# Expert weights of a two-layer backbone: ring of five tiles of each kind, two down tiles to a slot, the next unit's first three tiles fetched in the running unit

## The chip, the cores and the metric

The kernel runs on one core of one Trainium2 chip. The metric is the device time of one execution in microseconds. Three executions of the kernel before took 1493.27, 1498.73 and 1499.72 us (median 1498.73).

## The reference, cut to what matters

The program is one inference step of a two-layer backbone for 128 context tokens and 128 latent tokens of width 1024, all in 32-bit floats. Layer 0 mixes with a gated linear recurrence beside latent attention and a dense SwiGLU; layer 1 mixes with a bidirectional RWKV-7 recurrence and ends in a mixture of eight experts, two of which each token uses. Only that last part is touched:

```
def swiglu(x, wg, wu, wd):
    return (jax.nn.silu(x @ wg) * (x @ wu)) @ wd

def moe_swiglu(x, w_router, wg, wu, wd):     # 8 experts, D_FF_EXPERT = 2816
    logits = (xt @ w_router).astype(jnp.float32)
    top_v, top_i = lax.top_k(logits, TOP_K)                      # TOP_K = 2
    top_w = jax.nn.softmax(top_v, axis=-1)
    gate = jnp.sum(jax.nn.one_hot(top_i, N_EXPERTS) * top_w[..., None], axis=1)
    for e in range(N_EXPERTS):
        out = out + gate[:, e:e + 1] * swiglu(xt, wg[e], wu[e], wd[e])
```

## The kernel before, in words

The experts' stage works in units. A unit is one expert with up to 86 (CAP) of its tokens; there are as many units as experts (8) plus one for each expert that more tokens chose, a number that the kernel finds at run time and writes into a small table (TBL). With these inputs there are 8 units. The hidden width 2816 is cut into 22 tiles of 128 (HB). For tile t a unit needs one gate/up weight tile (1 MB, `("gu", t)`) and one down weight tile (0.5 MB, `("d", t)`).

TensorE's order in a unit (function `unit`, lines 1683 to 1771): gate/up 0 with the transposition of the previous unit's outputs between its halves (line 1666), gate/up 1, down 0, the slots (line 1673); then a hardware loop over LOOPS = 5 passes of ROWS = 4 tiles, each tile being gate/up t and then down t-1; then the gather of the next unit's tokens (line 1656) and down 21. Line 1691 is the matmul of gate and up (64 matmul records a tile), line 1715 that of down (32 records a tile). Units 1 to 6 are one hardware loop around this (line 1778), unit 0 and the last unit have code of their own. In unit 0 the first two passes of four tiles are written out and the loop runs from the third. ScalarE takes the silu (line 2252), VectorE the product (line 3216). Results alternate between two buffers by the parity of t.

SyncE issues every weight transfer (`expert_tiles`, lines 576 to 603), in the order of UNIT_TILES: gu 0, gu 1, d 0, then gu t and d t-1 in turn, then d 21. The weights go to 11 slots of 1 MB each ("ring"). Slots 0, 1 and 2 are kept for gu 0, gu 1 and for d 0 and d 21 (one half each); the other eight turn over, four for gate/up and four for down tiles, each down tile using half of its slot. SyncE waits before each transfer until both halves of TensorE's array have done with the tile that lies there (counters tile_used and tile_used0), then issues, and comes to the next tile in order. In unit 0 five tiles (gu 6, 7, 8 and d 5, 6; AHEAD) go to working arrays W6 to W9 that the layer before has left, once the residual is ready ("x" at 6). Counters slot3, slot4, ... tell TensorE that a slot's tile has landed.

Of the kernel before, what the change touches and what calls it, by code (L numbers as in the profile page):

```python
# [28 lines left out]
P = 128  # L29
# [19 lines left out]
ROWS, LOOPS = 4, 5  # L49
# [76 lines left out]
UNIT_TILES = [("gu", 0), ("gu", 1), ("d", 0)]  # L126
# [5 lines left out]
def moe_slot(kind, t):  # L132
    if kind == "gu":
        return EXPERTS[t if t < 2 else 3 + 2 * ((t - 2) % ROWS)]
    return EXPERTS[2 if t in (0, HB - 1) else 4 + 2 * ((t - 1) % ROWS)]


def moe_free(kind, t):

    taken = up_taken if kind == "gu" else down_taken  # L140
    if kind == "gu":
        return taken(t) - UT if t < 2 else taken(t - ROWS) if t >= 2 + ROWS else taken(t + ROWS * (LOOPS - 1)) - UT
    if t in (0, HB - 1):
        return taken(t) - UT
    return taken(t - ROWS) if t > ROWS else taken(t + ROWS * (LOOPS - 1)) - UT

# [49 lines left out]
def program(nc, t, out):  # L198
    ctx = ExitStack()
    with ctx:  # L200
# [210 lines left out]
        AHEAD = {("gu", ROWS + 2 + n): W[6 + n][:, :] for n in range(3)}  # L411
        AHEAD.update({("d", ROWS + 1 + n): W[9][:, n * D:(n + 1) * D] for n in range(2)})
        AHEAD_SLOTS = [moe_slot(kind, b) for kind, b in AHEAD]
        AHEAD_LANDED = 16 * (2 + len(AHEAD))
# [88 lines left out]
        def _(sp):  # L503
# [72 lines left out]
            def expert_tiles(u, e):  # L576

                for n, (kind, b) in enumerate(UNIT_TILES):
                    slot = ring[:, moe_slot(kind, b), :]
                    if kind == "gu":  # L580
                        dst, src = slot, t["moe_gu"][bass.ds(e, 1), b].rearrange("a p n -> (a p) n")
                    else:
                        dst = slot[:, D:2 * D] if b == HB - 1 else slot[:, 0:D]
                        src = t["moe_w_down"][0][bass.ds(e, 1), b * P:(b + 1) * P, :].rearrange("a k n -> (a k) n")
                    if u is None and (kind, b) in AHEAD:
                        sp.wait_ge(sem("x"), 6)
                        sp.dma_start(AHEAD[kind, b], src).then_inc(sem("x_in"), 16)
                        continue
                    free = n - RING + 1 if u is None and n < RING else moe_free(kind, b)
                    if u is None and (kind, b - ROWS) in AHEAD:  # L590
                        free = (up_taken if kind == "gu" else down_taken)(b - 2 * ROWS)
                    at = N_MOE + free if u is None else u * UT + (N_MOE + free)
                    sp.wait_ge(sem("tile_used"), at)
                    sp.wait_ge(sem("tile_used0"), at)
                    last = kind == "d" and b == HB - 1
                    sp.dma_start(dst, src).then_inc(sem("slot_last" if last else f"slot{moe_slot(kind, b)}"), 16)

            expert_tiles(None, 0)
            with sp.Fori(1, NE - 1) as u:
                expert_tiles(u, u)  # L600
            sp.wait_ge(sem("table"), 1)
            with sp.Fori(NE - 1, sp.value_load(TBL[0:1, UNITS:UNITS + 1], min_val=NE, max_val=UNITS)) as u:
                expert_tiles(u, sp.value_load(TBL[0:1, bass.ds(u, 1)], min_val=0, max_val=NE - 1))
# [89 lines left out]
        def _(pe):  # L693
# [985 lines left out]
            due0 = list(walk.due)  # L1679

            def unit(u, prev=None, rows=False):
# [13 lines left out]
                def gate_up(t, due, between=lambda: None, ahead=None):  # L1695

                    slot = moe_slot("gu", t)
                    if ahead is None:
                        pe.wait_ge(sem(f"slot{slot}"), due)
                    else:  # L1700
                        pe.wait_ge(sem("x_in"), AHEAD_LANDED)
                    w = (ring[:, slot, :] if ahead is None else ahead).rearrange("p (w k n) -> p w k n", w=2, k=KC)
                    across(bank[t % 2], w[:, 0])
                    between()
                    across(bank[2 + t % 2], w[:, 1])

                def down(t, arrived, due, hid, ahead=None):

                    if ahead is None:
                        pe.wait_ge(sem(arrived), due)  # L1710
                    pe.wait_ge(sem("hid"), hid)
                    half = D if t == HB - 1 else 0
                    w = ring[:, moe_slot("d", t), half:half + D] if ahead is None else ahead
                    for c in range(KC):
                        ins = [mm(bank[4 + c // 4][hp, (c % 4) * CAP:(c % 4 + 1) * CAP],  # L1715
                                  w[:, c * P + hp.start:c * P + hp.stop], HIDU[:, t % 2, :],
                                  start=t == 0 and c % 4 == 0, stop=t == HB - 1, skip_group_check=True) for hp in HALVES]
                        if prev is not None and t == HB - 1 and c % 4 == 3:
                            ins[0].then_inc(sem("last_down"), 1)
                            ins[1].then_inc(sem("last_down"), 1)  # L1720
                    if prev is None or t < HB - 1:
                        taken(ins)
# [8 lines left out]
                def once(slot):  # L1731
                    return u * 16 + (due0[slot] + 16)

                pe.wait_ge(sem("xg"), u * 2 + 2)
                gate_up(0, once(moe_slot("gu", 0)), outputs_turned)
                gate_up(1, once(moe_slot("gu", 1)))
                down(0, f"slot{moe_slot('d', 0)}", once(moe_slot("d", 0)), u * HB + (FT + 1))
# [9 lines left out]
                def due(slot, i, skipped):  # L1747

                    return u * (16 * LOOPS) + i * 16 + (due0[slot] + 16 - (16 if skipped and slot in AHEAD_SLOTS else 0))

                def steps(i, skipped, ahead={}):

                    for t in range(2, 2 + ROWS):
                        slot, slot_d = moe_slot("gu", t), moe_slot("d", t - 1)
                        gate_up(t, due(slot, i, skipped), ahead=ahead.get(("gu", t + ROWS)))
                        down(t - 1, f"slot{slot_d}", due(slot_d, i, skipped), u * HB + i * ROWS + (FT + t),
                             ahead.get(("d", t - 1 + ROWS)))

                if first_of_all:
                    steps(0, False)  # L1760
                    steps(1, False, AHEAD)
                with pe.Fori(2 if first_of_all else 0, LOOPS) as i:
                    steps(i, True)
# [7 lines left out]
                down(HB - 1, "slot_last", u * 16 + 16, u * HB + (FT + HB))  # L1771
# [22 lines left out]
        def _(act):  # L1794
# [448 lines left out]
            def unit(u, prev=None, rows=False):  # L2243
# [21 lines left out]
                with act.Fori(0, LOOPS) as i:  # L2265
                    for t in range(2, 2 + ROWS):
                        silu(t, u * UT + i * (3 * ROWS) + (N_MOE + gate_taken(t)), u * HB + i * ROWS + (FT + t - 1))
# [1118 lines left out]
```

## Time and profile before

| | |
|---|---|
| median of three executions | 1498.73 us |
| profiled execution | 1498.9 us, span 1497.0 us, mean granted clock 0.996 |
| TensorE busy | 1433.6 us, 96% |
| VectorE, ScalarE, GpSimd busy | 529.7, 303.5, 38.7 us |
| moved by DMA | 413.76 MB, mean 276 GB/s |
| lines 1691 and 1715, the experts' matmuls | 450.2 and 237.2 us busy |

The span is the time from the first to the last instruction of the profiled execution. Of the chain of work that ended last, 91% is TensorE, and 43% is lines 1691 and 1715. Busy times of TensorE overlap in part, since matmuls of the two halves of the array run together: 64 records of 238 ns take 2.39 us. Among the DMA queues q1 carries the weights, q0 the transfers of GpSimd, q8 and q14 are named "instruction".

### The profile page before, as it was taken

The numbers are of one execution on the slowest core, as the hardware profiler recorded it, in microseconds if no ns is written. First come the engines' busy times: TensorE is split into PE (matmuls) and PEld (weight loads), VectorE is DVE, ScalarE is ACT, GpSimd is POOL, SyncE is SP. The second block draws the span as 40 slices with busy tenths as digits, with TensorE's granted clock in tenths as the row PEclk, the third lists the DMA queues.
The fourth block names the chain that finished last, engine by engine and source line by source line (L and its number), as shares of the span: only waits on it lengthen the run. The fifth ranks groups of instructions, "written<-read, shape, count | busy, mean of one in ns | idle before, by whom it ended". The sixth has DMA issues, their size and how long they took to land.

```text
span 1497.0 us, 60951 instructions
## 1 busy us (share of the span) xinstructions
PE 1433.6 (96%) x27147; PEld 1274.0 (85%) x27147; DVE 529.7 (35%) x1496; ACT 303.5 (20%) x870; POOL 38.7 (3%) x59
## 2 busy tenths in 40 slices
PE   5999999999999999999999899999999999999997
PEld 3888588999547787888778899999999999999896
DVE  1474427666636355788623210000101010010012
ACT  2112423000102523455342010100101010000101
POOL 0100000000000000100000000000000000000000
PEclk9999999999999999999999999999999999999999
DMA  9823849544448132100185999999999999999995
GB/s 390 321 95 123 308 170 396 196 170 169 179 180 330 57 127 87 35 8 7 48 283 219 378 397 403 417 417 418 399 418 399 419 417 417 417 403 417 394 414 212
DMA packets 77441, 413.76 MB, mean 276 GB/s; under 512 B 12920, under 2 KB 13354, under 8 KB 40452
## 3 DMA queue, kind: packets, MB, share of 16 engines
q1 hardware_dynamic: 68752, 399.96, 67.4%
q0 software_dynamic: 7456, 9.56, 2.2%
q8 instruction: 98, 1.61, 0.4%
q10 hardware_dynamic: 1108, 2.41, 0.4%
q14 instruction: 27, 0.22, 0.0%
HBM read 407.50 MB, written 6.48 MB: 277 GB/s over the span
## 4 chain that ended last, share of the span: by engine, by line
PE 91%; DVE 3%; DMA 2%; ACT 2%; issue 1%; ACTq 0%; DVEq 0%; SPq 0%
PE banks L1691 29%; PE banks L1715 14%; PE banks L1070 9%; PE banks L1109 4%; PE banks L718 3%; PE banks L721 3%; PE banks L824 3%; PE banks L827 3%; PE banks L1236 2%; PE banks L1295 2%; PE banks L744 2%; PE banks L1656 1%; PE banks L1313 1%; PE banks L860 1%; PE banks L1324 1%
## 5 line engine op out<-in xcount | busy, mean ns | idle before, releaser
L1691 PE MATMUL banks<-w,ring 128*64 128x86 f32 x11072 | 450.2, 238 | 8.1 <-issue 5.1
L1691 PEld LDWEIGHTS banks<-w,ring 128*64 128x64 f32 x11072 | 426.6, 136 | 18.9 <-issue 7.5
L3216 DVE TENSOR_TENSOR w<-w,banks 128x86 f32<-128x86 f32 x176 | 43.1, 245 | 566.5 <-PE banks L1691 558.4
L1715 PE MATMUL banks<-w,ring 128*64 128x86 f32 x5568 | 237.2, 238 | 1.7 <-issue 1.5
L1715 PEld LDWEIGHTS banks<-w,ring 128*64 128x64 f32 x5568 | 219.4, 137 | 2.0 <-issue 2.0
L2252 ACT ACTIVATE w<-banks 128x86 f32<-128x86 f32 x176 | 42.7, 242 | 587.7 <-PE banks L1691 587.7
L718 PE MATMUL banks<-w,ring 128*128 128x256 f32 x224 | 49.2, 380 | 0.6 <-issue 0.3
L744 PE MATMUL banks<-ring,ct 128*32 128x256 f32 x768 | 47.3, 395 | 2.3 <-ACT ct L1818 2.1
L721 PE MATMUL banks<-ring,w 128*128 128x256 f32 x224 | 48.9, 379 | 0.0
L718 PEld LDWEIGHTS banks<-w,ring 128*128 128x128 f32 x224 | 42.3, 190 | 7.4 <-issue 1.8
L721 PEld LDWEIGHTS banks<-ring,w 128*128 128x128 f32 x224 | 42.3, 190 | 5.9 <-DVE w L2334 0.2
L1070 PE MATMUL banks<-w 128*128 128x128 f32 x352 | 43.0, 275 | 0.6 <-DVE w L2608 0.6
L824 PE MATMUL banks<-ht,ring 128*128 128x256 f32 x192 | 43.5, 383 | 0.0
L1070 PE MATMUL banks<-ht,ring 128*128 128x128 f32 x352 | 43.0, 275 | 0.0
L1070 PE MATMUL banks<-w,ring 128*128 128x128 f32 x352 | 42.9, 275 | 0.0
L744 PEld LDWEIGHTS banks<-ring,ct 128*32 128x32 f32 x768 | 23.6, 113 | 22.4 <-issue 6.6
L1109 PE MATMUL banks<-ring,w 128*128 128x512 f32 x88 | 42.2, 592 | 0.0
L827 PE MATMUL banks<-ring,ht 128*128 128x256 f32 (+1 forms) x192 | 42.0, 372 | 0.0
L1070 PEld LDWEIGHTS banks<-w 128*128 128x128 f32 x352 | 41.1, 192 | 0.8 <-DVE w L2608 0.8
L1070 PEld LDWEIGHTS banks<-ht,ring 128*128 128x128 f32 x352 | 41.1, 192 | 0.4 <-issue 0.4
L1070 PEld LDWEIGHTS banks<-w,ring 128*128 128x128 f32 x352 | 41.1, 192 | 0.0
L824 PEld LDWEIGHTS banks<-ht,ring 128*128 128x128 f32 x192 | 35.8, 190 | 5.2
(481 smaller groups left out, 1747.2 us busy)
## 6 DMA issues: line engine op xcount, KB each, us to landing
ring<-in_moe_gu SPq DMA_DIRECT2D x173, 1024.0 KB, 12.1
ring<-in_moe_w_down SPq DMA_DIRECT2D x174, 512.0 KB, 12.2
ring<-in_ada_w SPq DMA_DIRECT2D x48, 1024.0 KB, 5.2
ring<-in_ev_w_in SPq DMA_DIRECT2D x11, 1024.0 KB, 27.1
ring<-in_ffn_w_gate SPq DMA_DIRECT2D x11, 1024.0 KB, 12.4
ring<-in_ffn_w_up SPq DMA_DIRECT2D x11, 1024.0 KB, 10.8
ring<-in_ffn_w_down SPq DMA_DIRECT2D x11, 1024.0 KB, 6.4
ring<-in_ev_w_out SPq DMA_DIRECT2D x4, 1024.0 KB, 6.8
```

Source lines behind the costliest of these rows:

```text
L718: ins = mm(b[:, a * TW:(a + 1) * TW], w[:, k, a * P:(a + 1) * P], src[:, k, :], start=k == 0, stop=k == KC - 1)
L721: ins = mm(b[:, a * TW:a * TW + n], src[:, k, a * P:(a + 1) * P], w[:, k, 0:n], start=k == 0, stop=k == KC - 1)
L744: ins = mm(sums_bank(n)[32 * q:32 * q + 32, 0:TW], CT[:, NST * k:NST * k + 32], w[:, k % 2, q * TW:(q + 1) * TW], start=k == 0, stop=k == ...
L824: ins = mm(b[:, a * TW:(a + 1) * TW], w[:, k, a * P:(a + 1) * P], HT[:, k, :], start=k == 0, stop=k == KC - 1)
L827: ins = mm(b[:, a * TW:a * TW + n], HT[:, k, a * P:(a + 1) * P], w[:, k, 0:n], start=k == 0, stop=k == KC - 1)
L1070: ins = mm(region(j, r)[:, which * P:(which + 1) * P], lhs(which, k), rhs(k), start=first and which == 0 and k == 0, stop=k == 3, skip_gro ...
L1109: ins = mm(bank[DOWN_BANK[p]][:, :], lhs, rhs, start=n == 0, stop=n == FT - 1)
L1236: ins = mm(bank[7 - n % 2][:, a * TW:(a + 1) * TW], XS["v"][:, k, a * P:(a + 1) * P], held["w"][:, k, :], start=k == 0, stop=k == KC - 1)
L1691: ins = [mm(b[hp, 0:CAP], w[:, k, hp], XG[:, k, :], start=k == 0, stop=k == KC - 1, skip_group_check=True) for hp in HALVES]
L1715: ins = [mm(bank[4 + c // 4][hp, (c % 4) * CAP:(c % 4 + 1) * CAP], w[:, c * P + hp.start:c * P + hp.stop], HIDU[:, t % 2, :], start=t == 0 ...
L2252: A(SILU[:, t % 2, :], bank[t % 2][:, 0:CAP], ACT.Silu).then_inc(sem("silu"), 1)
L3216: v.tensor_tensor(HIDU[:, t % 2, :], SILU[:, t % 2, :], bank[2 + t % 2][:, 0:CAP], ALU.mult).then_inc(sem("hid"), 1)
```

## The change

- The ring's eight turning slots (3 to 10) are dealt anew: gate/up tiles take slots 3, 5, 6, 8 and 9 in turn, down tiles take slot 4 twice (both halves), slot 7 twice and slot 10 once. Five tiles of each kind turn over.
- Five does not divide the alternation by two buffers, so the hardware loop's body is ROUNDS x ROWS = 10 tiles, run LOOPS = 2 times, in unit 0 as well (no passes written out), on TensorE and on ScalarE.
- SyncE issues the next unit's gu 0, gu 1 and d 0 inside the running unit, behind its d 5, d 6 and d 7 (EARLY), each once its slot is free. To know the next unit's expert it reads the table twice a unit, and it waits for the table ahead of unit 1. The last unit has code of its own without the early tiles.
- No tiles go to the arrays W6 to W9 any more.
- Each half of a shared slot has a landing counter of its own (moe_landed).

The diff, without renamed helper calls that follow from it:

```
-ROWS, LOOPS = 4, 5
+ROWS, ROUNDS, LOOPS = 5, 2, 2
...
-UNIT_TILES = [("gu", 0), ("gu", 1), ("d", 0)]
+FIRST_TILES = [("gu", 0), ("gu", 1), ("d", 0)]
+UNIT_TILES = []
 for _t in range(2, HB):
     UNIT_TILES += [("gu", _t), ("d", _t - 1)]
 UNIT_TILES += [("d", HB - 1)]
 
 
 def moe_slot(kind, t):
+
     if kind == "gu":
-        return EXPERTS[t if t < 2 else 3 + 2 * ((t - 2) % ROWS)]
-    return EXPERTS[2 if t in (0, HB - 1) else 4 + 2 * ((t - 1) % ROWS)]
+        return EXPERTS[t if t < 2 else (3, 5, 6, 8, 9)[(t - 2) % ROWS]]
+    return EXPERTS[2 if t in (0, HB - 1) else (4, 4, 7, 7, 10)[(t - 1) % ROWS]]
+
+
+def moe_half(t):
+
+    return 1 if t == HB - 1 or t and (t - 1) % ROWS in (1, 3) else 0
+
+
+def moe_landed(kind, t):
+
+    if kind == "d" and moe_half(t):
+        return "slot_last" if t == HB - 1 else f"half{(t - 1) % ROWS // 2}"
+    return f"slot{moe_slot(kind, t)}"
 
 
 def moe_free(kind, t):
 
     taken = up_taken if kind == "gu" else down_taken
     if kind == "gu":
-        return taken(t) - UT if t < 2 else taken(t - ROWS) if t >= 2 + ROWS else taken(t + ROWS * (LOOPS - 1)) - UT
+        return taken(t) - UT if t < 2 else taken(t - ROWS) if t >= 2 + ROWS else taken(t + ROWS * (ROUNDS * LOOPS - 1)) - UT
     if t in (0, HB - 1):
         return taken(t) - UT
-    return taken(t - ROWS) if t > ROWS else taken(t + ROWS * (LOOPS - 1)) - UT
-
-
+    return taken(t - ROWS) if t > ROWS else taken(t + ROWS * (ROUNDS * LOOPS - 1)) - UT
+
+
+
+EARLY = {("d", ROWS): (("gu", 0), up_taken(0)), ("d", ROWS + 1): (("gu", 1), up_taken(1)),
+         ("d", ROWS + 2): (("d", 0), down_taken(0))}
...
-        AHEAD = {("gu", ROWS + 2 + n): W[6 + n][:, :] for n in range(3)}
-        AHEAD.update({("d", ROWS + 1 + n): W[9][:, n * D:(n + 1) * D] for n in range(2)})
-        AHEAD_SLOTS = [moe_slot(kind, b) for kind, b in AHEAD]
-        AHEAD_LANDED = 16 * (2 + len(AHEAD))
...
-            def expert_tiles(u, e):
-
-                for n, (kind, b) in enumerate(UNIT_TILES):
-                    slot = ring[:, moe_slot(kind, b), :]
-                    if kind == "gu":
-                        dst, src = slot, t["moe_gu"][bass.ds(e, 1), b].rearrange("a p n -> (a p) n")
-                    else:
-                        dst = slot[:, D:2 * D] if b == HB - 1 else slot[:, 0:D]
-                        src = t["moe_w_down"][0][bass.ds(e, 1), b * P:(b + 1) * P, :].rearrange("a k n -> (a k) n")
-                    if u is None and (kind, b) in AHEAD:
-                        sp.wait_ge(sem("x"), 6)
-                        sp.dma_start(AHEAD[kind, b], src).then_inc(sem("x_in"), 16)
-                        continue
-                    free = n - RING + 1 if u is None and n < RING else moe_free(kind, b)
-                    if u is None and (kind, b - ROWS) in AHEAD:
-                        free = (up_taken if kind == "gu" else down_taken)(b - 2 * ROWS)
-                    at = N_MOE + free if u is None else u * UT + (N_MOE + free)
-                    sp.wait_ge(sem("tile_used"), at)
-                    sp.wait_ge(sem("tile_used0"), at)
-                    last = kind == "d" and b == HB - 1
-                    sp.dma_start(dst, src).then_inc(sem("slot_last" if last else f"slot{moe_slot(kind, b)}"), 16)
-
-            expert_tiles(None, 0)
-            with sp.Fori(1, NE - 1) as u:
-                expert_tiles(u, u)
+            def expert_tile(kind, b, e, at):
+
+                slot = ring[:, moe_slot(kind, b), :]
+                if kind == "gu":
+                    dst, src = slot, t["moe_gu"][bass.ds(e, 1), b].rearrange("a p n -> (a p) n")
+                else:
+                    dst = slot[:, moe_half(b) * D:(moe_half(b) + 1) * D]
+                    src = t["moe_w_down"][0][bass.ds(e, 1), b * P:(b + 1) * P, :].rearrange("a k n -> (a k) n")
+                sp.wait_ge(sem("tile_used"), at)
+                sp.wait_ge(sem("tile_used0"), at)
+                sp.dma_start(dst, src).then_inc(sem(moe_landed(kind, b)), 16)
+
+            loaded = set()
+
+            def free_at(u, kind, b):
+
+                place = EXPERTS.index(moe_slot(kind, b)), moe_half(b) if kind == "d" else 0
+                if isinstance(u, int) and place not in loaded:
+                    loaded.add(place)
+                    return N_MOE + place[0] - RING + 1
+                return u * UT + (N_MOE + moe_free(kind, b))
+
+            def expert_tiles(u, e, following=None):
+
+                for kind, b in UNIT_TILES:
+                    expert_tile(kind, b, e, free_at(u, kind, b))
+                    if following is not None and (kind, b) in EARLY:
+                        first, taken = EARLY[kind, b]
+                        expert_tile(*first, following, u * UT + (N_MOE + taken))
+
+            for kind, b in FIRST_TILES:
+                expert_tile(kind, b, 0, free_at(0, kind, b))
+            expert_tiles(0, 0, 1)
             sp.wait_ge(sem("table"), 1)
-            with sp.Fori(NE - 1, sp.value_load(TBL[0:1, UNITS:UNITS + 1], min_val=NE, max_val=UNITS)) as u:
-                expert_tiles(u, sp.value_load(TBL[0:1, bass.ds(u, 1)], min_val=0, max_val=NE - 1))
+            last = sp.value_load(TBL[0:1, UNITS + 1:UNITS + 2], min_val=NE - 1, max_val=UNITS - 1)
+            with sp.Fori(1, last) as u:
+                expert_tiles(u, sp.value_load(TBL[0:1, bass.ds(u, 1)], min_val=0, max_val=NE - 1),
+                             sp.value_load(TBL[0:1, bass.ds(u + 1, 1)], min_val=0, max_val=NE - 1))
+            expert_tiles(last, sp.value_load(TBL[0:1, bass.ds(last, 1)], min_val=0, max_val=NE - 1))
...
-                def gate_up(t, due, between=lambda: None, ahead=None):
-
-                    slot = moe_slot("gu", t)
-                    if ahead is None:
-                        pe.wait_ge(sem(f"slot{slot}"), due)
-                    else:
-                        pe.wait_ge(sem("x_in"), AHEAD_LANDED)
-                    w = (ring[:, slot, :] if ahead is None else ahead).rearrange("p (w k n) -> p w k n", w=2, k=KC)
+                def gate_up(t, due, between=lambda: None):
+
+                    pe.wait_ge(sem(moe_landed("gu", t)), due)
+                    w = ring[:, moe_slot("gu", t), :].rearrange("p (w k n) -> p w k n", w=2, k=KC)
                     across(bank[t % 2], w[:, 0])
                     between()
                     across(bank[2 + t % 2], w[:, 1])
 
-                def down(t, arrived, due, hid, ahead=None):
-
-                    if ahead is None:
-                        pe.wait_ge(sem(arrived), due)
+                def down(t, due, hid):
+
+                    pe.wait_ge(sem(moe_landed("d", t)), due)
                     pe.wait_ge(sem("hid"), hid)
-                    half = D if t == HB - 1 else 0
-                    w = ring[:, moe_slot("d", t), half:half + D] if ahead is None else ahead
+                    w = ring[:, moe_slot("d", t), moe_half(t) * D:(moe_half(t) + 1) * D]
...
+                def once(kind, t):
+                    return u * 16 + (due0[moe_landed(kind, t)] + 16)
+
+                def in_turn(kind, t, i):
+                    turn = (t - (2 if kind == "gu" else 1)) // ROWS
+                    return u * (16 * ROUNDS * LOOPS) + i * (16 * ROUNDS) + (due0[moe_landed(kind, t)] + 16 * turn + 16)
 
                 pe.wait_ge(sem("xg"), u * 2 + 2)
-                gate_up(0, once(moe_slot("gu", 0)), outputs_turned)
-                gate_up(1, once(moe_slot("gu", 1)))
-                down(0, f"slot{moe_slot('d', 0)}", once(moe_slot("d", 0)), u * HB + (FT + 1))
+                gate_up(0, once("gu", 0), outputs_turned)
+                gate_up(1, once("gu", 1))
+                down(0, once("d", 0), u * HB + (FT + 1))
                 if not first_of_all:
                     pe.wait_ge(sem("unit_yg"), u * 2)
                     pe.sem_inc(sem("settled"), 1)
@@ -1744,23 +1767,10 @@
                     ins.then_inc(sem("selt_done"), 1)
                 elif not first_of_all:
                     slots(bank[6], SEL, TOKENS)
-                def due(slot, i, skipped):
-
-                    return u * (16 * LOOPS) + i * 16 + (due0[slot] + 16 - (16 if skipped and slot in AHEAD_SLOTS else 0))
-
-                def steps(i, skipped, ahead={}):
-
-                    for t in range(2, 2 + ROWS):
-                        slot, slot_d = moe_slot("gu", t), moe_slot("d", t - 1)
-                        gate_up(t, due(slot, i, skipped), ahead=ahead.get(("gu", t + ROWS)))
-                        down(t - 1, f"slot{slot_d}", due(slot_d, i, skipped), u * HB + i * ROWS + (FT + t),
-                             ahead.get(("d", t - 1 + ROWS)))
-
-                if first_of_all:
-                    steps(0, False)
-                    steps(1, False, AHEAD)
-                with pe.Fori(2 if first_of_all else 0, LOOPS) as i:
-                    steps(i, True)
+                with pe.Fori(0, LOOPS) as i:
+                    for t in range(2, 2 + ROUNDS * ROWS):
+                        gate_up(t, in_turn("gu", t, i))
+                        down(t - 1, in_turn("d", t - 1, i), u * HB + i * (ROUNDS * ROWS) + (FT + t))
...
-                    for t in range(2, 2 + ROWS):
-                        silu(t, u * UT + i * (3 * ROWS) + (N_MOE + gate_taken(t)), u * HB + i * ROWS + (FT + t - 1))
+                    for t in range(2, 2 + ROUNDS * ROWS):
+                        silu(t, u * UT + i * (3 * ROUNDS * ROWS) + (N_MOE + gate_taken(t)), u * HB + i * (ROUNDS * ROWS) + (FT + t - 1))
```

## Rows read from the trace of the kernel before

**Rows 1.** The page: span, busy time by engine, instruction queue q8.

```profile
span 1497.0 us, 60951 instructions
...
PE 1433.6 (96%) x27147; PEld 1274.0 (85%) x27147; DVE 529.7 (35%) x1496; ACT 303.5 (20%) x870; POOL 38.7 (3%) x59
...
q8 instruction: 98, 1.61, 0.4%
```

**Rows 2.** Chain of waits (start us, us, what): starts of units, gathers, last down tile.

```profile
798.87 5.00 PE banks L1691 x128
...
881.47 2.54 PE banks L1656 x64
...
966.28 2.39 PE banks L1656 x64
...
1137.54 2.39 PE banks L1656 x64
...
1220.54 2.39 PE banks L1656 x64
...
1389.14 2.39 PE banks L1656 x64
...
1480.81 1.83 PE banks L1715 x48
```

**Rows 3.** Chain of waits: a tile in two stretches, units 2 and 4.

```profile
1099.87 2.58 PE banks L1691 x64
...
1163.15 2.39 PE banks L1691 x64
1165.54 1.19 PE banks L1715 x32
```

**Rows 4.** Stretches: busy us and records by engine, granted clock, DMA share, GB/s.

```profile
1060.00:1080.00 20.00, 20.00 (x532) 19.88 (x530) 2.23 (x10) 1.46 (x6) 1.22 (x1) 1.00 0.99 381
1100.00:1120.00 20.00, 20.00 (x514) 19.27 (x514) 1.23 (x5) 1.21 (x5) 0.00 (x0) 1.00 1.02 417
1180.00:1200.00 20.00, 20.00 (x544) 20.00 (x542) 2.08 (x10) 1.21 (x5) 0.00 (x0) 1.00 1.02 418
...
1420.00:1440.00 20.00, 17.42 (x411) 16.91 (x409) 0.98 (x4) 1.02 (x5) 1.52 (x2) 0.91 1.00 407
```

**Rows 5.** Chain of waits in unit 0.

```profile
827.00 1.44 issue
...
833.42 1.56 issue
```

**Rows 6.** Chain of waits in unit 7.

```profile
1406.37 1.41 issue
...
1412.71 1.53 issue
...
1435.71 4.25 PE banks L1691 x64
```

**Rows 7.** DMA queues (packets, MB, share) in 798:882, 882:970, 970:1390, 1390:1450 us.

```profile
q8 instruction: 11, 0.18, 0.8%
...
q8 instruction: 6, 0.10, 0.5%
...
DMA packets 34974, 173.46 MB, mean 413 GB/s; under 512 B 6587, under 2 KB 6587, under 8 KB 21019
...
q8 instruction: 4, 0.07, 0.4%
```

**Rows 8.** Stretches: the first 20 us of unit 0.

```profile
800.00:820.00 20.00, 20.00 (x543) 20.00 (x541) 6.60 (x29) 2.74 (x7) 0.00 (x0) 1.00 0.22 70
```

**Rows 9.** Waits of SyncE's queue, 970 to 1390: total us, times, longest.

```profile
SPq L594 <- PE banks L1691: 223.0, 94, 13.1
```

**Rows 10.** Groups of instructions, TensorE, 1051.9 to 1137.5: count, busy us, mean ns.

```profile
L1666 PE MATMUL banks<-cst,w 128*86 128x128 f32 x8 | 1.0, 274 | 0.0
L1673 PE MATMUL banks<-w 128*86 128x3 f32 x4 | 0.5, 222 | 0.0
```

More of the change, by code:

```diff
@@ L1677, in _ @@
             gather(SEL0)
-            due0 = list(walk.due)
+            due0 = {f"slot{n}": landed for n, landed in enumerate(walk.due)}
+            due0.update(half0=0, half1=0, slot_last=0)
             def unit(u, prev=None, rows=False):
@@ L1729, in outputs_turned @@
                     turn_y("y_turned")
-                def once(slot):
-                    return u * 16 + (due0[slot] + 16)
+                def once(kind, t):
[3 more added lines that the diff above has]
+                    return u * (16 * ROUNDS * LOOPS) + i * (16 * ROUNDS) + (due0[moe_landed(kind, t)] + 16 * turn + 16)
                 pe.wait_ge(sem("xg"), u * 2 + 2)
-                gate_up(0, once(moe_slot("gu", 0)), outputs_turned)
-                gate_up(1, once(moe_slot("gu", 1)))
-                down(0, f"slot{moe_slot('d', 0)}", once(moe_slot("d", 0)), u * HB + (FT + 1))
+                gate_up(0, once("gu", 0), outputs_turned)
+                gate_up(1, once("gu", 1))
+                down(0, once("d", 0), u * HB + (FT + 1))
                 if not first_of_all:
@@ L1770, in unit @@
                     gather(SEL)
-                down(HB - 1, "slot_last", u * 16 + 16, u * HB + (FT + HB))
+                down(HB - 1, once("d", HB - 1), u * HB + (FT + HB))
             unit(0, rows=True)
```

## The prediction, made before the changed kernel was run

> **What bounds the kernel now.** I read the page first, then the stretches, the chain of waits, and last the DMA queues. The reader is to see TensorE busy for 96% of the span [rows 1], so a change pays only by what it takes out of TensorE's own chain. The experts' stage starts at 798.9 us and ends at 1482.6 us [rows 2], 684 of the 1497 us; nothing before it is touched. It has eight units.
>
> In a stretch where TensorE waits for nothing a tile costs 2.39 + 1.19 = 3.58 us (64 matmuls of gate and up, 32 of down); elsewhere the same tile takes 2.58 + 1.19 = 3.77 us [rows 3]. Both stretches have the DMA at 417 to 418 GB/s [rows 4]. A tile is 1.5 MB, 1.573e6 bytes; over 417 GB/s that is 3.77 us. So the slow pace is the transfers', and the fast one TensorE's. A unit without any wait is 22 x 3.58 + 2.39 (gather) + 1.0 (turned outputs) + 0.5 (slots) = 82.6 us [rows 2, 3, 10], and its 34.6 MB need 83.0 us of transfer. The two are level, and the ring between them decides what each loses: right behind a unit's start the transfer rate falls to 381 GB/s for 20 us [rows 4], because the ring is full while TensorE eats the first three tiles, which free nothing that the queue wants next. TensorE pays for this later at the slow pace.
>
> From one gather to the next unit 1 takes 84.8 us, units 2 and 3 together 171.3, unit 4 83.0, units 5 and 6 together 168.6 [rows 2]; against 82.6 each they lose 2.2, 6.1, 0.4 and 3.4. Unit 0, from its first matmul to the gather, takes 82.6 where 22 x 2.39 + 21 x 1.19 + 0.5 = 78.1 are work: 4.5 lost. Unit 7, from the gather to the end of the last down matmul, takes 93.5 against 82.6 + 1.2 = 83.8: 9.7 lost. Together 26 us. The profiled execution took 1498.9 us (span 1497.0), 0.2 above the median of 1498.73; with no such loss it would take 1473.
>
> **A second kind of wait.** Not all of the 26 us is for data. In unit 0 and unit 7 TensorE stands still in the middle of a run of matmuls of one line, 1.44, 1.56, 1.41 and 1.53 us, with nothing released ("issue") [rows 5, 6]. The instruction queue q8 explains it. It moved 98 packets, 1.61 MB, in the whole run [rows 1]. TensorE executed 2 x 27147 = 54294 instructions, but 14780 of the matmuls are repeats of loop bodies (768 in unit 0, 1536 each in units 1 and 7, 5 x 2188 in units 2 to 6), which leaves 12367, or 24734 instructions that are new. 1.61 MB over those is 65 bytes each, 252 to a packet. So q8 brings TensorE's code, every block once. Units 2 to 6 run with no q8 packet at all (the queue has no row there), units 0 and 1 and the first 60 us of unit 7 with 11, 6 and 4 [rows 7]: code in a loop is kept. In unit 7 the stalls begin 1406.37 and 1412.71, 6.3 us apart, where a block holds 126 matmuls, 4.7 us. So a fetch under a full transfer queue takes about 6.3 us and is asked for one block ahead. With the DMA at 70 GB/s TensorE passes its new blocks without a gap (20.00 us busy of 20) [rows 8].
>
> **The change, part by part.**
> *Ring.* Five tiles of each kind turn over instead of four, so the queue can be one tile (3.6 us) further ahead. The next unit's first three tiles, 2.62 MB or 6.3 us of transfer, go into the queue behind down tiles 5, 6 and 7. That delays gate/up 7 and what follows by 6.3 us; the cover is the lead from the boundary, where TensorE works 2.39 + 1.19 + 1.0 + 0.5 + 2 x 2.39 + 1.19 = 11.0 us on work whose weights are already there. 11.0 - 6.3 - 20 x 0.19 = 0.9 us remains at the unit's end, so no data wait is left. If that cover failed, a tile would come up to 6.3 us late once per unit, 44 us over seven. Worth of this part: the data's share of the 26 us, at most 15 (6.1 + 0.4 + 3.4 and about 5 of unit 7), at least 0.
> *Arrays.* Five tiles no longer go to the idle arrays ahead of unit 0. Before, 9 gate/up and 7 down tiles, 13.1 MB, came ahead of the first matmuls, and in the 20 us from 800 the DMA then moved only 70 GB/s, 1.4 MB [rows 8]. Now 7 gate/up tiles and 6 down halves, 10.5 MB, come first; the next unit's gate/up 0 follows when the first tile is used (802) and the ring's next tiles from 808 on, when gate/up 2 is used: by 820 that is 10.5 + 1.0 + 12 x 0.417 = 16.5 MB against 14.5. No loss, some 5 us of lead gained.
> *SyncE.* Two value loads a unit and a wait for the table (made in unit 0's tile 12) now stand ahead of unit 1. SyncE spent at least 223 of 420 us waiting for slots in units 2 to 6 [rows 9]; nothing is behind these but transfers that wait anyway: 0.
> *ScalarE and GpSimd.* The same activations in a body of ten; 0.
> *TensorE's code.* Ten tiles (odd rings of five, buffers that alternate by two) are now one loop body, where there were four. Old inner body: 4 x 96 = 384 matmuls, 768 instructions, 3.0 blocks. A unit executes 22 x 96 + 64 + 8 + 4 = 2188 matmuls [rows 2, 3, 10], of which 16 x 96 are repeats; the old unit body is 652 matmuls, 1304 instructions, 5.2 blocks, the longest code that this trace shows to be kept. New inner body: 960 matmuls, 1920 instructions and some 20 for waits, 7.7 blocks, 126 KB; new unit body 1228 matmuls, 9.8 blocks, 161 KB. No row shows 7.7 or 9.8 blocks kept. The cost lies between nothing (all kept) and a fetch of every block in every pass. I take the second as likeliest, because the new unit body is nearly twice the longest that is shown, and nothing speaks for a memory without an end.
>
> [...]
>
> *Price if nothing is kept.* A jump back to a missing block costs one fetch. Lower end 1.0 us, the packet itself (0.8% of 16 engines' 84 us over 11 packets [rows 7]); upper end 6.3. Transfers will still fill some 85% of the time, so I take 4.2. The target's rest lasts half a block on average, 2.35 us, and the next block again takes 4.2: 1.85 more. A stop that long may drop the clock: behind the one wait of 2.4 us in unit 7 the granted clock averages 0.91 over its 20 us, and 64 matmuls take 4.25 instead of 2.39 [rows 4, 6]; I take half of 1.86, 0.9. Together 7.0 us a jump. There are 8 inner jumps (two passes a unit) and 5 outer ones (units 1 to 6): 13 x 7.0 = 91 us. The blocks run through in sequence: 4376 instructions a unit and some 50 for waits are 17.5 blocks, 140 in all, 127 without the targets. Each waits 0 (quiet) to 1.6 us (full queue). TensorE at 3.58 against transfers at 3.77 a tile fills the queue again, until TensorE loses 0.19 a tile, 0.25 a block; I take that: 32 us. Sum 123 us; 1473 + 123 = 1596 us. Its own range: with 2.5 us a jump and nothing else 1473 + 33 = 1506; with 6.3 + 3.9 + 1.9 a jump and 0.6 a block 1473 + 157 + 76 = 1706.
>
> **The rivals.**
> *Inner body kept, unit body not.* Then 5 outer jumps, 35 us, and some 10 blocks a unit in sequence, 80 in all. With one stop a unit the queue is fuller, so between 0.25 and 1.6 each, I take 0.6: 48 us. 1473 + 83 = 1556 us (1500 to 1620). For it: 7.7 blocks is only 1.5 times what is shown. [...]
> *All kept: the change does what it says, and the result is not slower.* What decides is whether 161 KB stay; if so, no jump costs anything. Each block is fetched once; units 1 and 7 have 9.8 new blocks instead of 5.2 under a full queue, where 5.2 cost 2.2 and about 3.1: up to 1.5 more for each of 4.6, I take 7 us a unit. With 4.5 for unit 0 and 2 of data waits some 21 us remain of the 26: 1473 + 21 = 1494 us, 5 faster (1486 to 1502). For it: no row shows where the memory ends, and repeats up to 5.2 blocks are free.
> *The early tiles starve the middle of a unit.* Priced above at 44 us if the cover fails; the 11 us lead speaks against it, and it would only add to the last case: 1538 us.
>
> **How the numbers follow.** Nothing kept 0.46 (1596), inner kept 0.25 (1556), all kept 0.26 (1494), starving 0.03 (1538). A difference below 0.5%, 7.5 us, cannot be told from none. The all-kept case reaches below 1491.4 in half of its chance, 0.13; the rest is "same", 0.12 and 0.01 from the next case. Slower: 0.74. The range goes down to 1490, which leaves out a third of the all-kept case (0.09), and up to 1660, which leaves out about a fifth of the likeliest (0.10). The likeliest case alone spans 1506 to 1706.
>
> **What would show it.** In units 2 to 6 the queue q8, empty now, would show 17 to 19 packets a unit if nothing is kept, some 10 if the inner body is, none if all is; in the whole run about 220, 160 or 106 instead of 98. The chain would show "issue" stops of 3 to 6 us once in the middle of a unit and once at its start, a granted clock below 1 behind them, and shorter stops every block. DMA over units 2 to 6 would fall from 413 to some 350 GB/s. The slow data pace of 2.58 us for 64 matmuls should be gone. I am wrong if q8 stays empty in these units; then the ring decides, and the time is near 1494. I am wrong in size if the stops at the jumps are near 1 us.

## The result, and the profile after

The changed kernel takes 1695.13 us (median of 4 runs, 1692.06 to 1702.6) against 1497.2 (4 runs): a ratio of 1.133, 95% interval 1.130 to 1.135. I forecast slower, 1596 us with a range up to 1660. The likeliest case was the right one, and I forecast for it half of what came: +97 us against +198.

The page after (span; busy time by engine; the instruction queue; the chain's shares), to be read against [rows 1]:

```profile
span 1692.7 us, 60862 instructions
...
PE 1480.8 (87%) x27147; PEld 1310.4 (77%) x27147; DVE 529.9 (31%) x1496; ACT 304.4 (18%) x870; POOL 38.7 (2%) x59
...
q8 instruction: 238, 3.90, 0.9%
...
PE 84%; issue 10%; DVE 2%; ACT 2%; DMA 1%; ACTq 0%; DVEq 0%
```

TensorE executes the same 27147 matmuls, and q8 brings 238 packets of code instead of 98. 10% of the chain is now "issue". One unit alone (1121.4 to 1230.7 us) has this row, where the same unit had none in [rows 7]:

```profile
q8 instruction: 21, 0.34, 1.3%
```

What TensorE waited for in the experts' stage (us in total, times, longest):

```profile
PE banks L1716 <- issue: 132.2, 78, 5.5
PE banks L1734 <- issue: 18.5, 19, 1.6
PE banks L1680 <- issue: 9.2, 6, 2.2
```

There is no row of a wait for a weight tile; all 160 us are "issue", and the experiments show that they are for code. Lines 1716, 1734 and 1680 are the old 1691, 1715 and 1656. The chain of waits, whose lines are start, length and what (x is the number of matmuls), at the turn from unit 3 to unit 4 (1231.56), and in the middle of unit 4:

```profile
1227.90 1.13 issue
1229.03 1.34 PE banks L1680 x25
1230.37 1.19 PE banks L1734 x16
1231.56 4.91 issue
1236.47 2.26 PE banks L1716 x27
1238.73 0.78 issue
...
1241.96 5.21 PE banks L1716 x96
...
1264.12 1.65 issue
...
1275.40 1.50 PE banks L1716 x40
1276.89 1.27 issue
1278.16 1.12 PE banks L1716 x24
...
1280.46 2.39 PE banks L1716 x64
...
1293.04 4.91 issue
1297.95 4.85 PE banks L1716 x64
```

Each part of the story is here: a jump that costs 4.91 us at the unit's start, the next block late by 0.78, a block in sequence late by 1.65, the inner jump with 4.91 again, and behind it 64 matmuls that take 4.85 us where they took 2.39 [rows 3]. Away from the stops 64 matmuls take 2.39 us again: the slow pace of 2.58 is gone. A tile with a stop in it needs 1.50 + 1.12 = 2.62 us of matmuls, so a stop in a tile costs 0.23 us beside its own length. The stretches around it, with granted clock, DMA share and GB/s as the last three columns:

```profile
1232.00:1242.00 10.00, 4.76 (x42) 3.86 (x44) 0.60 (x2) 0.93 (x3) 0.00 (x0) 0.64 0.03 10
1242.00:1255.00 13.00, 13.00 (x300) 12.87 (x302) 1.74 (x8) 1.41 (x4) 1.40 (x1) 0.88 0.48 154
1255.00:1292.00 37.00, 29.97 (x777) 29.18 (x775) 2.00 (x9) 1.94 (x8) 0.00 (x0) 1.00 1.00 391
```

During the jump the transfers stand (10 GB/s: SyncE issues nothing from 1226.80 to 1244.67 and waits up to 17.2 us for TensorE to free a slot) and the granted clock falls to a mean of 0.64: it is 0.50 from the end of the stop at 1236.47 to 1245, and 1.00 again behind that. Afterwards the transfers run at 391 GB/s, and there TensorE is busy for only 30 of 37 us, at a granted clock of 1.00.

The whole stage, from the first matmul of unit 0 to the last down tile, is one row:

```profile
798.90:1681.00 882.10, 721.89 (x17440) 697.18 (x17441) 78.04 (x316) 62.80 (x210) 11.45 (x9) 0.95 0.81 310
```

882 us against 684 before [rows 2]: the stage holds all of the loss.

### The profile page after: what moved, and what is told of

The parts are those of the page before. It is cut to its first block, busy times and chain, and to the rows that moved or that the text cites. A ratio compares the mean times of both kernels' runs of the same rounds, so it can differ in the third digit from the quotient of the medians.

```text
span 1692.7 us, 60862 instructions
## 1 busy us (share of the span) xinstructions
PE 1480.8 (87%) x27147; PEld 1310.4 (77%) x27147; DVE 529.9 (31%) x1496; ACT 304.4 (18%) x870; POOL 38.7 (2%) x59
## 4 chain that ended last, share of the span: by engine, by line
PE 84%; issue 10%; DVE 2%; ACT 2%; DMA 1%; ACTq 0%; DVEq 0%
PE banks L1716 28%; PE banks L1734 13%; PE banks L1094 8%; PE banks L1133 4%; PE banks L742 3%; PE banks L745 3%; PE banks L848 3%; PE banks L851 2%; PE banks L1260 2%; PE banks L1319 1%; PE banks L1680 1%; PE banks L768 1%; PE banks L1337 1%; PE banks L884 1%; PE banks L1348 1%
## 5 line engine op out<-in xcount | busy, mean ns | idle before, releaser
L1716 PE MATMUL banks<-w,ring 128*64 128x86 f32 x11264 | 501.5, 245 | 132.8 <-issue 132.2
L1716 PEld LDWEIGHTS banks<-w,ring 128*64 128x64 f32 x11264 | 469.4, 142 | 149.4 <-issue 148.2
L1734 PE MATMUL banks<-w,ring 128*64 128x86 f32 x5632 | 257.5, 240 | 18.6 <-issue 18.5
L1734 PEld LDWEIGHTS banks<-w,ring 128*64 128x64 f32 x5632 | 236.2, 139 | 22.4 <-issue 22.0
```

Of the source, the lines that this page charges most:

```text
L1716: ins = [mm(b[hp, 0:CAP], w[:, k, hp], XG[:, k, :], start=k == 0, stop=k == KC - 1, skip_group_check=True) for hp in HALVES]
```

## The experiments

**Code made short, everything else kept.** The ring of five, the shared slots and the early tiles stay; the loop body is five tiles, four times.

```
-ROWS, ROUNDS, LOOPS = 5, 2, 2
+ROWS, ROUNDS, LOOPS = 5, 1, 4
...
+def buf(t):
+
+    return t if t < 2 else (0, 1, 0, 1, 2)[(t - 2) % ROWS]
...
+        GATE = [bank[0][:, 0:CAP], bank[1][:, 0:CAP], bank[7][:, 0:CAP]]
+        UP = [bank[2][:, 0:CAP], bank[3][:, 0:CAP], bank[6][:, 256:256 + CAP]]
...
-                    across(bank[t % 2], w[:, 0])
+                    across(GATE[buf(t)], w[:, 0])
...
+                    pe.wait_ge(sem("hid"), u * HB + (FT + HB))
                     gather(SEL)
```

The wait in the last lines is new: the gather writes the bank that the last product reads. In every pass but a unit's first the first down tile reads the array of another tile, so this kernel, like e5 and e6 below, leaves out one right product in five. The number and the sizes of its matmuls and transfers do not depend on that.

> The changed kernel with its ring, slots and early tiles as they are, but a loop body of five tiles run four times instead of ten tiles run twice: a third set of buffers (bank 7 for gate, bank 6 for up, a third silu and product array) serves every fifth tile, and the gather waits for the product of tile 21. The unit body shrinks from 1228 matmuls (9.8 blocks of code) to 748 (6.0 blocks). Theory A (TensorE's code is fetched again in each pass because the bodies no longer fit): q8 falls from 238 packets to about 100, the stops vanish, and the time falls below the kernel before, 1475 to 1490 us, since the larger ring is what is left. Rival B (the new arrangement of slots and the early tiles cost the time by themselves): still 1650 to 1700 us. Rival C (code is half of it): 1550 to 1600.

1494.8 us, ratio to the kernel before 0.9986 (0.9977 to 0.9995), q8:

```profile
q8 instruction: 94, 1.54, 0.4%
```

With the same ring and the same order of transfers the whole loss is gone (e9, with the right products, takes 1495.2). Rivals B and C fall. What I expected of the larger ring (down to 1475) did not come either.

**The old ring with long code.** TensorE's loop over five passes is written out:

```
-                if first_of_all:
-                    steps(0, False)
-                    steps(1, False, AHEAD)
-                with pe.Fori(2 if first_of_all else 0, LOOPS) as i:
-                    steps(i, True)
+                for i in range(LOOPS):
+                    steps(i, i > 1 if first_of_all else True, AHEAD if first_of_all and i == 1 else {})
```

> The kernel before with its ring of four, its order of transfers and its idle arrays, but TensorE's twenty tiles of a unit written out one after another: no inner loop, a unit body of 17.3 blocks. Theory A: every unit fetches all of its code, q8 shows about 210 to 230 packets, and with 1.3 us a block and one jump a unit the time is 1620 to 1670 us, though nothing of the ring was changed. Rival B (ring and order are the cause): as the kernel before, 1490 to 1510 us.

1641.6 us (one run). Page and stage row:

```profile
q8 instruction: 223, 3.65, 0.9%
```

```profile
798.90:1628.00 829.10, 698.19 (x17424) 677.47 (x17419) 77.94 (x316) 62.37 (x210) 11.45 (x9) 0.97 0.85 328
```

Nothing of the changed ring is in this kernel, and long code alone costs 144 us. Only TensorE's code is longer, and q8 goes from 98 packets to 223: what q8 brings is TensorE's code. It has one jump a unit instead of two: its five jump stops take 29 us (5.6 to 6.1 each) and its 87 others 102 us. Together with e1 this settles the cause from both sides.

**Where the memory for code ends.** One pass of four tiles is written out in front of the inner loop, in the unit loop alone:

```
+                elif prev is None:
+                    for i in range(1):
+                        steps(i, True)
-                with pe.Fori(2 if first_of_all else 0, LOOPS) as i:
+                with pe.Fori(2 if first_of_all else 1 if prev is None else 0, LOOPS) as i:
```

> The kernel before, with the first of the five passes of a unit written out in the unit loop: the unit body grows from 5.2 to 8.2 blocks, the inner loop stays at 3.0. If the memory for code ends near 8 blocks: the outer body is fetched again in every unit (about 8 or 9 packets each for five units, q8 near 145), the inner loop is kept, and the time is 1540 to 1580 us. If it is clearly larger (10 blocks and more, so that only the ten-tile unit body is too long): q8 near 101 packets and 1500 us.

1557.3 us (one run). The page, and then one unit (975 to 1070 us):

```profile
q8 instruction: 151, 2.47, 0.6%
```

```profile
q8 instruction: 10, 0.16, 0.7%
```

A unit body of 8.2 blocks is fetched again in every unit. An inner body of 3.0 blocks inside it is not: it runs four passes, and the unit has only ten packets. e1's unit body of some 6.0 blocks is kept (from 1115 to 1206 us q8 has no packet). The inner body of the changed kernel, 7.7 blocks, is not: 21 packets a unit are both passes. So the end lies between 6.0 and 7.7 blocks of 252 instructions as counted here. Which block is given up when was not tried.

**What a jump and a block cost apart from the transfers.** The changed kernel (e4) and the kernel before (e8) run with small expert transfers, and e11 lies between; all three leave out a part of the weights, while TensorE's work stays as it is:

```
-                sp.dma_start(dst, src).then_inc(sem(moe_landed(kind, b)), 16)
+                sp.dma_start(dst[:, 0:512], src[:, 0:512]).then_inc(sem(moe_landed(kind, b)), 16)
```

> The changed kernel with every expert weight transfer cut to the first 512 columns of its tile (a quarter of a gate/up tile, half of a down tile), so two thirds of the experts' bytes are left out and most of the weights are stale; TensorE's work and waits are unchanged. It takes the load off the DMA and leaves the code fetches. If a fetch is slow because it stands behind the weights: the stops in sequence vanish, a jump costs 1.5 to 3 us, q8 still shows 238 packets, time 1510 to 1550 us. If a fetch takes 5 to 6 us of its own: the stops stay and the time stays at 1650 to 1700 us.

> The kernel before with every expert weight transfer cut to its first 512 columns, as in e4 (the rest of each tile is left out). TensorE without any wait for data and with kept code: the floor from which e4 is read. Theory: the 26 us of waits in the stage go, 1471 to 1476 us, q8 98 packets. The difference to e4 is then 13 jumps, their cold clock and nothing else: some 90 us, 7 a jump. If the floor is near 1497 the pace of 3.77 us a tile was not the transfers'.

1565.4 us for the changed kernel and 1473.9 for the kernel before, one run each. Stage rows, first the changed kernel with small transfers:

```profile
798.90:1551.00 752.10, 693.11 (x17434) 682.97 (x17430) 77.95 (x316) 61.96 (x209) 11.45 (x9) 0.95 0.41 128
```

and the kernel before with small transfers:

```profile
798.90:1458.00 659.10, 657.64 (x17404) 653.92 (x17400) 77.38 (x315) 61.13 (x208) 11.47 (x9) 1.00 0.45 141
```

The second is the floor, 659 us of 659 busy, and 1474 in all, as the prediction's accounts had it (1473). The first lies above my expected 1510 to 1550. TensorE's waits in it, and a part of its chain:

```profile
PE banks L1716 <- issue: 58.9, 24, 4.2
```

```profile
1265.44 3.07 issue
1268.51 1.25 PE banks L1716 x27
1269.76 1.50 issue
...
1316.25 4.01 issue
1320.26 4.25 PE banks L1716 x64
```

24 waits are left of 103: the 13 jumps with 47 us, and 11 blocks with 12 us, six of them right behind a jump. Together they stand for 59 us, 4.5 a jump. TensorE's busy time is 693 instead of 658, 35 us more or 2.7 a jump. The granted clock can explain it: 0.95 on average over 752 us is worth at most 38 us. 752 - 659 = 93 us over 13 jumps are 7.2 each. So even with the DMA at 41% a jump stops TensorE for 2.9 to 4.2 us, and most of the waiting in sequence is gone.

e11 is the changed kernel with `dst[:, 0:1024], src[:, 0:1024]` in the same line.

> The changed kernel with every gate/up transfer cut to half of its columns and the down transfers whole: 1.0 instead of 1.5 MB a tile, 2.5 us of transfer beside 3.58 us of matmuls; a third of the experts' bytes are left out. It tells what makes a fetch in sequence late. If a fetch is late only where the transfer queue stays full for longer than TensorE needs for a block (4.7 us), the queue empties once a tile here and the stops in sequence stay nearly out: 1565 to 1590 us, and the changed kernel's 1 us a block is the price of a queue that is full between its pauses. If the wait grows in proportion to the bytes moved: about half of 130 us stays, 1615 to 1640 us.

1616.7 us (one run), between the two, and in the range of the proportional answer:

```profile
798.90:1602.00 803.10, 709.21 (x17441) 692.52 (x17438) 77.95 (x316) 62.17 (x210) 11.45 (x9) 0.94 0.68 230
```

The stage of the three kernels against the floor, with TensorE's stops read off their chains and waits (us):

| | DMA share | above the floor | stops at the 13 jumps | stops elsewhere (count) | TensorE busy longer by |
|---|---|---|---|---|---|
| e4 | 0.41 | 93 | 47 | 12 (11) | 35 |
| e11 | 0.68 | 144 | 57 | 35 (42) | 52 |
| changed kernel | 0.81 | 223 | 60 | 100 (90) | 64 |

The stops elsewhere are 0.1, 0.3 and 0.8 us for each of the 127 blocks in sequence, and the 0.23 us beside a stop come on top: by this estimate 21 us in the changed kernel, 1.0 a block in all. The other 43 us of its longer busy time fit the granted clock (0.95 over 882 us is worth at most 44). The price of a block rises with the load at each step that was run, and no step shows where it begins.

**The order of the transfers.** In e7 the first three tiles go back to the head of the next unit:

```
-                    if following is not None and (kind, b) in EARLY:
-                        first, taken = EARLY[kind, b]
+                if following is not None:
+                    for first, taken in EARLY.values():
                         expert_tile(*first, following, u * UT + (N_MOE + taken))
```

> The changed kernel with its ten-tile body, but the next unit's first three tiles at the head of the next unit. Code and jumps are as in the changed kernel (q8 238). If the stops between blocks come from transfers that are crowded into the middle of the unit by the early tiles, they shrink here: 1655 to 1685 us. If the order has no part in it: 1690 to 1700 us.

1707.5 us (one run): no better, and beyond the four runs of the changed kernel. My idea that the early tiles crowd the middle of the unit falls. In order the DMA is still busy when the outer jump comes (408 GB/s in the 4.5 us before it, 325 in the 5.5 us before the changed kernel's). The five outer stops take 4.4 to 6.0 us, against 2.4 to 4.9 in the changed kernel; the one at 1240.49:

```profile
1240.49 5.97 issue
```

The same edit with short code (e6, e10). The short code also gets its slots copied early (e5, e6, e9, e10), and its buffers dealt anew so that every down tile reads its own product (e9, e10):

```
+                    v.tensor_copy(SLOTS, bank[6][0:CAP, 0:3]).then_inc(made("dve_chain"), 1)
...
-    return t if t < 2 else (0, 1, 0, 1, 2)[(t - 2) % ROWS]
+    return t if t < 2 else (0, 1, 2, 0, 1)[(t - 2) % ROWS]
```

> The five-tile body once more, with one edit: VectorE copies the three slot columns out of bank 6 at the start of a unit, before gate and up of the fifth tiles use that bank. One small copy per unit beside TensorE's work. Theory (code was all of the loss, and the larger ring with early tiles moves nothing by itself, because the transfers already fill their time): within 0.5% of the kernel before, 1492 to 1497 us, q8 94 packets. Rival (the larger ring does pay): below 1490 us.

> As the last, but the next unit's first three tiles are issued at the head of the next unit, in the order in which TensorE uses them, instead of behind down tiles 5, 6 and 7. What the early order alone is worth. Theory (what counts is that the DMA never stands, and at the unit's start the early order leaves it with nothing to fetch): 0 to 6 us faster than the early order, 1488 to 1495 us. Rival (early tiles help): 2 to 6 us slower, 1497 to 1501 us.

> The five-tile body with its three sets of buffers dealt so that the body's first down tile reads what the body's last tile wrote (0, 1, 2, 0, 1; in e1 and e5 that one product in five came from another tile's array, so a part of the down products was wrong there, with the same instructions). Only positions change, and the gather waits for nothing new. Theory: as e1 and e5, 1492 to 1497 us. If the mended buffers bring a wait of their own: above 1497.

> The same with the next unit's first three tiles at the head of the next unit. Theory: the order in which the tiles are used leaves the DMA something to fetch at the start of a unit; as e6, 1488 to 1492 us, 0.3 to 0.6% below the kernel before. If the gain of e6 hung on its wrong buffers: 1495 and more.

| kernel | median us | ratio to before, 95% interval |
|---|---|---|
| e5, early | 1495.17 | 0.9977 (0.9964 to 0.9991) |
| e6, in order | 1490.9 | 0.9946 (0.9933 to 0.9960) |
| e9, early, right buffers (0, 1, 2, 0, 1) | 1495.24 | 0.9988 (0.9977 to 0.9998) |
| e10, in order, right buffers | 1489.63 | 0.9946 (0.9932 to 0.9960) |

All four came as expected. e10 is 0.5% faster than the kernel before. The kernel before fetches in order as well, from a ring of four, so the ring of five pays once the early tiles are taken out. Why the order matters is in the transfer rate. e9 over 970 to 1390 us, then e10 over 971.7 to 1387.6:

```profile
DMA packets 34900, 173.18 MB, mean 412 GB/s; under 512 B 6578, under 2 KB 6578, under 8 KB 20949
```

```profile
DMA packets 34935, 173.25 MB, mean 417 GB/s; under 512 B 6583, under 2 KB 6583, under 8 KB 20995
```

The kernel before had 413 [rows 7]. With early tiles the queue runs short once a unit has started. In e9 unit 4 starts at 1141, the transfers keep 411 to 428 GB/s up to 1149.5, and then:

```profile
1150.50:1153.00 2.50, 2.50 (x74) 2.50 (x72) 0.24 (x1) 0.17 (x1) 0.00 (x0) 1.00 0.53 171
```

The kernel before lost rate in the same place [rows 4]. In e10 no stretch of 2.5 us in the first 22 us of units 3 and 4 is below 391 GB/s, and the two units take 83.2 and 83.0 us, which is the time of 34.6 MB at 417 GB/s:

```profile
1054.60:1137.80 83.20, 83.19 (x2194) 82.46 (x2192) 8.10 (x34) 7.52 (x27) 1.41 (x1) 1.00 1.02 417
1137.80:1220.80 83.00, 83.00 (x2194) 82.41 (x2192) 8.10 (x34) 7.52 (x27) 1.41 (x1) 1.00 1.02 417
```

## Why the prediction was right in direction and wrong in size

- **Base.** "With no such loss it would take 1473": e8 measured 1473.9. Right.
- **The fetch, read from the kernel before.** 1.61 MB in 98 packets are 16.4 KB each, and between the stops at 1406.37 and 1412.71 [rows 6] TensorE executes 127 matmuls, 254 instructions against the 252 to a packet of the prediction. That a block is asked for one ahead, while TensorE works in the one before it, shows in the times of the packets. In the quiet start of unit 0 one moves in each of the stretches 802 to 804, 808 to 810, 812 to 814 and 818 to 820 us while TensorE is never idle [rows 8]; in unit 7 they start at 1405.3 and 1411.7, some 1 us before the stops at 1406.37 and 1412.71; in the changed kernel the packet behind the jump stop that ends at 1297.95 starts at 1298.4. The 6.3 us of a fetch under load are an estimate from stops 6.3 us apart; e2's jump stops of 5.6 to 6.1 us come near it. That a jump costs one fetch fits the changed kernel's stops of 4.91 us at 1231.56 and 1293.04, in each of which one packet starts (1233.9, 1295.2); in the one of 4.85 us at 1346.32 two do (1346.8, 1347.8).
- **Nothing kept.** Its chance of 0.46 against the 0.25 of "inner body kept" was my estimate, since no row shows more than 5.2 blocks in a loop. Forecast "about 220" packets, 17 to 19 a unit; 238 and 21 came. Right, shown by e1, e2 and e3. e3 stands for the rival "inner body kept, unit body not" in small, and shows that it was a real possibility: its inner body of 3.0 blocks stayed. 7.7 blocks were too many.
- **Blocks in sequence: the step that failed.** "TensorE at 3.58 against transfers at 3.77 a tile fills the queue again, until TensorE loses 0.19 a tile, 0.25 a block; I take that: 32 us." With the late block behind each jump (13 x 1.85 = 24) the forecast has 56 us for late blocks. The changed kernel has 90 such stops with 100 us, and an estimated 21 beside them: 121 us, 1.0 a block. Of the 99 us that the forecast missed (1695 - 1596) this step is some 65. The error was to take the pace that would make transfers and matmuls level as the price. It holds only if the transfers are spread evenly, and they are not: while TensorE stands at a jump and works through the unit's first tiles the DMA moves 10 and 154 GB/s, and then it runs at 391 for the next 37 us. That stretch has five stops of 1.2 to 1.7 us, 7.0 us over its 6.2 blocks (777 matmuls) or 1.1 each, and two thirds of a unit run at such rates (383 GB/s from 1306 to 1346). e2, with one jump a unit, pays as much in sequence (102 us in 87 stops) with the stage's DMA share at 0.85 instead of 0.81, fuller as the rival with one stop a unit had it. That the bunching sets the price fits this and is not shown by itself, since no run spreads the transfers evenly. e11 shows that the price is not zero below saturation (35 us in 42 stops at a share of 0.68). I had written down the upper end, 1.6 a block, but let the range end with 0.6; with 1.6 the likeliest case would have reached 1473 + 91 + 203 = 1767 and held the result.
- **Jumps.** The stop itself was right: 4.2 forecast, 4.6 measured (60 us over 13). The low clock was the second term that was too small: "I take half of 1.86, 0.9", 12 us in all, where about 43 came, some 31 of the 99. In e4 and in the changed kernel the clock falls behind every jump, not behind half of them, and costs about 3 us each time. The forecast of 13 x 7.0 = 91 us meets the 93 of e4 by luck: e4 has the DMA at 41%, the forecast was made for 85%, and its parts (4.2, 1.85, 0.9) were not those measured there (3.6 for the stop, 0.9 for other stops, 2.7 for longer matmuls).
- **Ring.** At most 15 us, at least 0: the ring of five with early tiles is worth 0.1% (e9). "No data wait is left" holds for the changed kernel, but there code slows TensorE; in e9 the slow pace (2.58 us for 64 matmuls) comes back in units 3 and 5. The lead of 11 us at a unit's start was to cover the early tiles. In the changed kernel the DMA moves 10 GB/s in the ten us from 1232, and in e9 it falls to 171 right behind the lead: what it could have fetched there had been fetched already.
- **Arrays, SyncE, ScalarE.** Priced at nothing. e9 has all three edits and is level with the kernel before, so no loss from them shows; apart from each other and from the ring they were not tried.
- **Starving.** No wait for a weight tile appears after the change, and tiles without a stop take 2.39 us instead of 2.58; the rival is out.

## What to carry to other kernels

Count the instructions of every loop body that a change makes longer, the outer ones too, and compare them with the longest body that the trace shows running without packets in the engine's instruction queue; here 6.0 blocks of 252 instructions were kept, and 7.7 and 8.2 were not. When code must be fetched in a loop, price each jump at its stop plus the low clock behind it (4.6 and about 3 us in the changed kernel), and each block in sequence by the load of the DMA in that stretch, not by its mean: between two pauses, with the DMA at a share of 1.00, a block cost 1.1 us here, where I had taken 0.25. And look at what a prefetch moved earlier leaves to the queue in the place that it was moved from: with early tiles the transfers fell to 171 GB/s behind a unit's start (e9), in order they stayed at 391 GB/s or more in the first 22 us of units 3 and 4, and the kernel was 0.4% faster (e10, 1489.6 us against 1495.2).

## What the runs showed of the hardware

- A jump to code that is not kept stops TensorE for 2.9 to 4.2 us with the DMA at a share of 0.41 (e4), for 2.4 to 5.5 us in the changed kernel, and for 5.6 to 6.1 us in e2. At each outer jump of the changed kernel TensorE executes 27 matmuls and then stops again, for 0.8 to 1.5 us; that the target lies near the end of its block would explain it and was not tried.
- After each of the 13 jumps of e4 and of the changed kernel the granted clock is down: it is 0.50 for 3.4 to 10.2 us and then 1.00 again. The 64 matmuls behind an inner jump take 3.7 to 4.9 us instead of 2.39 in units 0 to 6; in unit 7 a second stop falls among them. Of the stops in sequence those of 1.65 us and less in the chain above left it at 1.00 (stretch 1255 to 1292), while behind one of 2.48 us at 884.05 it was 0.50 from 886.6 to 890.0.
- Code of up to 6.0 blocks was fetched once, whatever the number of passes: e1 ran eight units of four passes with 94 packets, fewer than the 98 before.
